# Shorter inverse roots and a new order of steps behind feed-forward layers and in two mixers

## The reference

```
h = rms_norm(x);  proj = h @ w_in
mix = (sigmoid(g_a) * (rg_lru(...) @ w_rnn_out) + sigmoid(g_b) * (sparse_attention(...) @ w_att_out)) @ w_o
x = x + rms_norm(mix)                       # post norm of the mixer: "f0"
f = (silu(h @ w_gate) * (h @ w_up)) @ w_down        # h = rms_norm(x), width 2816
x = x + rms_norm(f)                         # post norm of the feed-forward layer: "f1"
```

## Time and profile before

| | |
|---|---|
| median of 3 runs | 1452.25 us (1450.88 to 1452.64) |
| the profiled execution: its own time, its span | 1452.73 us, 1450.9 us |
| PE busy | 1406.1 us, 97% of the span |
| DVE busy | 892.9 us, 62% |
| ACT busy | 770.1 us, 53% |
| DMA | 242.57 MB, mean 167 GB/s |
| granted clock of PE, mean | 0.985 of full speed |
| chain that ended last | PE 93%, DVE 3%, ACT 3%, issue 1% |

### The profile page before, as it was taken

How to read it: one execution, slowest core, us unless ns; L and a number is a source line. 1 busy time by engine, 2 the same in 40 slices (tenths; PEclk the granted TensorE clock), 3 DMA queues, 4 the chain that set the end, 5 groups by cost and what they waited for, 6 DMA issues and landing times.

```text
span 1450.9 us, 18581 instructions
## 1 busy us (share of the span) xinstructions
PE 1406.1 (97%) x6978; PEld 1183.1 (82%) x6978; DVE 892.9 (62%) x1429; ACT 770.1 (53%) x1153; POOL 14.0 (1%) x21
## 2 busy tenths in 40 slices
PE   6999999899998999999989999999999989999999
PEld 6798888788887788888768888888888868788887
DVE  6889756755555655558876555565555684555543
ACT  5589844554544444446755444444444585554442
POOL 2000000000000000000000000000000000000000
PEclk9999999999999999999999999999999999999999
DMA  8442566476654666565445665666656422366651
GB/s 285 130 132 79 175 221 182 139 210 186 186 188 134 189 189 185 182 187 174 157 127 179 188 177 187 188 188 187 182 183 189 142 88 73 88 191 186 189 186 62
DMA packets 131767, 242.57 MB, mean 167 GB/s; under 512 B 8544, under 2 KB 21472, under 8 KB 131680
## 3 DMA queue, kind: packets, MB, share of 16 engines
q1 hardware_dynamic: 130768, 239.15, 54.1%
q0 software_dynamic: 624, 2.10, 0.5%
q10 hardware_dynamic: 288, 0.14, 0.0%
HBM read 240.31 MB, written 1.05 MB: 166 GB/s over the span
## 4 chain that ended last, share of the span: by engine, by line
PE 93%; DVE 3%; ACT 3%; issue 1%; DMA 0%; SPq 0%; ACTq 0%; DVEq 0%
PE PB L345 27%; PE PB L347 27%; PE PB L346 27%; PE PB L385 5%; PE PB L610 2%; PE PB L499 2%; PE PB L339 1%; PE PB L341 1%; PE PB L340 1%; PE PB L503 0%; ACT JK L380 0%; DMA X<-in_x_dram 0%; PE PB L791 0%; DVE XC L777 0%; PE PB L980 0%
## 5 line engine op out<-in xcount | busy, mean ns | idle before, releaser
L318 DVE TENSOR_TENSOR WL<-RAW,WH 128x1024 fp32r<-128x1024 f32 (+1 forms) x453 | 549.7, 1218 | 458.9 <-ACT WH L312 458.7
L312 ACT ACTIVATE WH<-RAW 128x1024 fp32r<-128x1024 f32 (+1 forms) x453 | 476.8, 1054 | 538.7 <-PE PB L347 530.5
L345 PE MATMUL PB<-WH,AT0h 128*128 128x512 f32 (+3 forms) x1328 | 510.8, 385 | 13.0 <-DVE AT0l L1220 6.0
L347 PE MATMUL PB<-WH,AT0l 128*128 128x512 f32 (+3 forms) x1328 | 500.5, 377 | 0.0
L346 PE MATMUL PB<-WL,AT0h 128*128 128x512 f32 (+3 forms) x1328 | 500.2, 377 | 0.0
L345 PEld LDWEIGHTS PB<-WH,AT0h 128*128 128x128 f32 x1328 | 253.5, 191 | 60.5 <-issue 16.4
L346 PEld LDWEIGHTS PB<-WL,AT0h 128*128 128x128 f32 x1328 | 253.8, 191 | 44.6 <-issue 1.9
L347 PEld LDWEIGHTS PB<-WH,AT0l 128*128 128x128 f32 x1328 | 253.0, 191 | 45.5
L345 PE MATMUL PB<-WH,FTh 128*128 128x512 f32 x440 | 172.2, 391 | 0.0
L347 PE MATMUL PB<-WH,FTl 128*128 128x512 f32 x440 | 171.3, 389 | 0.0
L346 PE MATMUL PB<-WL,FTh 128*128 128x512 f32 x440 | 171.2, 389 | 0.0
(11 more groups left out here) (301 smaller groups left out, 1059.0 us busy)
## 6 DMA issues: line engine op xcount, KB each, us to landing
RAW<-in_ffn_w_gu_dram SPq DMA_DIRECT2D x88, 512.0 KB, 3.7
RAW<-in_ffn_w_gu_2b_dram SPq DMA_DIRECT2D x88, 512.0 KB, 3.7
RAW<-in_w_in_dram SPq DMA_DIRECT2D x48, 512.0 KB, 4.3
RAW<-in_ffn_w_down_dram SPq DMA_DIRECT2D x44, 512.0 KB, 3.3
RAW<-in_ffn_w_down_2b_dram SPq DMA_DIRECT2D x44, 512.0 KB, 3.4
...
```

What stands on the lines that cost most here:

```text
L312: e.activation(WH[i % NHL][:, 0:m], RAW[i % NRAW][:, 0:m], ACT.Copy).then_inc(*up("hi", i))
L318: e.tensor_tensor(WL[i % NHL][:, 0:m], RAW[i % NRAW][:, 0:m], WH[i % NHL][:, 0:m].bitcast(F32), ALU.subtract).then_inc(*up("lo", i))
L345: e.matmul(o, p.src[0][:, kx, t], h[:, j:j + p.n], start=start, stop=False)
L347: ins = e.matmul(o, p.src[1][:, kx, t], h[:, j:j + p.n], start=False, stop=stop)
```

## The change

It rewrites the root, cuts the post norm into three pieces, and moves calls in the lists of PE, ACT and DVE. Loads, tiles and semaphores stay as they are.

The root works on the sum, not on the mean; epsilon times the width goes into the addition of the partial sums where there is one, and the scale of the query heads (64 ** -0.5) into the constants. For one value per partition the two multiplications y * y * v are one instruction.

```diff
-        def inverse_root(e, v, y, t, n, name, key):
-            e.tensor_scalar(ti, vi, 1, None, ALU.logical_shift_right)
-            e.tensor_scalar(yi, ti, -1.0, float(0x5F3759DF), ALU.mult, ALU.add)
-            for r in range(3):
-                e.tensor_tensor(t, y, y, ALU.mult)
-                e.scalar_tensor_tensor(t, t, -0.5, v, ALU.mult, ALU.mult)
-                ins = e.scalar_tensor_tensor(y, t, 1.5, y, ALU.add, ALU.mult)
-        def rstd(e, v, y, t, n, width, name, key):
-            e.tensor_scalar(v, v, 1.0 / width, EPS, ALU.mult, ALU.add)
-            inverse_root(e, v, y, t, n, name, key)
+        def root(e, v, y, t, n, factor, name, key):
+            c = (factor * 3 / 256) ** (1 / 15)
+            bits = float(0x5F3759DF - 2 ** 31 - 130000 + round(float(np.log2(c)) * 2 ** 23))
+            e.tensor_scalar(t.bitcast(I32), v.bitcast(I32), 1, None, ALU.logical_shift_right)
+            e.tensor_scalar(y.bitcast(I32), t.bitcast(I32), -1.0, bits, ALU.mult, ALU.add)
+            for r in range(2):
+                if n == 1:
+                    e.tensor_scalar(t, y, y, v, ALU.mult, ALU.mult)
+                else:
+                    e.tensor_tensor(t, y, y, ALU.mult)
+                    e.tensor_tensor(t, t, v, ALU.mult)
+                if r == 0:
+                    e.scalar_tensor_tensor(y, t, -3 * c ** 2, y, ALU.add, ALU.mult)
+                else:
+                    e.scalar_tensor_tensor(t, t, -40 / 3 * c ** 6, t, ALU.add, ALU.mult)
+                    e.scalar_tensor_tensor(y, t, 80 * c ** 12, y, ALU.add, ALU.mult)
+        def rstd(e, v, y, t, n, width, name, key, factor=1.0):
+            e.tensor_scalar(v, v, width * EPS, None, ALU.add)
+            root(e, v, y, t, n, factor * width ** 0.5, name, key)
...
         def dve_rs(e, n):
-            e.tensor_tensor(SP[n], S2[n][:, 0:2], S2[n][:, 2:4], ALU.add)
-            rstd(e, SP[n], RS[n], TM[n], 2, D, "rs", n)
+            e.scalar_tensor_tensor(SP[n], S2[n][:, 0:2], D * EPS, S2[n][:, 2:4], ALU.add, ALU.add)
+            root(e, SP[n], RS[n], TM[n], 2, D ** 0.5, "rs", n)
```

PE's list:

```diff
 # behind WO[1], f0
             pe_turn_block(e, 'f0', 0, 1)
+            dense(e, F[0][0][0], 0, 1)
             pe_turn_block(e, 'f0', 1, 0)
+            dense(e, F[0][0][0], 1, 2)
             pe_turn_block(e, 'f0', 1, 1)
-            dense(e, F[0][0][0], 0, 8)
+            dense(e, F[0][0][0], 2, 8)
```

ACT's and DVE's lists follow: `act_exp`, `act_p`, `dve_max` and `dve_diff` move to where the new order of PE needs them, with `hi` and `lo` of the chunks between them. What the text below speaks of:

```diff
 # ACT, f1
             act_squares(e, 'f1', 1, 0)
-            act_squares(e, 'f1', 1, 1)
             act_block_hi(e, 'f1', 1, 0)
+            act_squares(e, 'f1', 1, 1)
 # ACT, even mixer, end
             hi(e, 233)
-            act_p(e, AT_B, 7)
+            act_sub(e, 1)
             hi(e, 234)
-            act_sub(e, 1)
+            act_out_hi(e, 'b', 1)
             act_squares(e, 'f2', 0, 0)
-            act_out_hi(e, 'b', 1)
 # ACT, odd mixer
             act_exp(e, AT_C, 0)
-            hi(e, 381)
+            act_exp(e, AT_C, 1)
             act_p(e, AT_C, 0)
             act_ukv(e, 0, 0)
...
             act_uq(e, 1, 1)
-            act_exp(e, AT_C, 1)
+            act_p(e, AT_C, 1)
             act_exp(e, AT_C, 2)
-            act_p(e, AT_C, 1)
 # DVE, f0
             lo(e, 74)
-            dve_post(e, 'f0', 0)
+            dve_post_root(e, 'f0', 0)
             lo(e, 75)
-            dve_post(e, 'f0', 1)
+            dve_post(e, 'f0', 0, 0)
+            dve_post(e, 'f0', 0, 1)
+            lo(e, 76)
+            dve_post_root(e, 'f0', 1)
             dve_block_lo(e, 'f0', 0, 0)
+            dve_post(e, 'f0', 1, 0)
+            dve_post(e, 'f0', 1, 1)
             dve_block_lo(e, 'f0', 0, 1)
+            lo(e, 77)
 # DVE, f1
-            dve_post(e, 'f1', 0)
+            dve_post_root(e, 'f1', 0)
             lo(e, 141)
+            dve_post(e, 'f1', 0, 0)
+            dve_post(e, 'f1', 0, 1)
+            lo(e, 142)
             dve_block_lo(e, 'f1', 0, 0)
-            dve_post(e, 'f1', 1)
+            dve_post_root(e, 'f1', 1)
             dve_block_lo(e, 'f1', 0, 1)
-            dve_rs(e, 'f1')
-            lo(e, 142)
-            dve_block_lo(e, 'f1', 1, 0)
+            dve_post(e, 'f1', 1, 0)
+            dve_post(e, 'f1', 1, 1)
             lo(e, 143)
             lo(e, 144)
+            dve_block_lo(e, 'f1', 1, 0)
+            dve_rs(e, 'f1')
             lo(e, 145)
             dve_block_lo(e, 'f1', 1, 1)
 # DVE, start of each mixer (210, 211 and 370, 371)
             dve_rs(e, 'od')
+            lo(e, 371)
             dve_x_lo(e, 'od', 2)
             dve_x_lo(e, 'od', 3)
-            lo(e, 371)
```

More of the change, by code:

```diff
@@ new lines, in root @@
+                if r == 0:
+                    e.scalar_tensor_tensor(y, t, -3 * c ** 2, y, ALU.add, ALU.mult).then_inc(*up("dve"))
+                else:
+                    e.scalar_tensor_tensor(t, t, -40 / 3 * c ** 6, t, ALU.add, ALU.mult).then_inc(*up("dve"))
+                    e.wait_ge(*last("dve"))
+                    e.scalar_tensor_tensor(y, t, 80 * c ** 12, y, ALU.add, ALU.mult).then_inc(*up(name, key))
+        def rstd(e, v, y, t, n, width, name, key, factor=1.0):
+            e.tensor_scalar(v, v, width * EPS, None, ALU.add).then_inc(*up("dve"))
@@ L370, in rstd @@
             e.wait_ge(*last("dve"))
-            inverse_root(e, v, y, t, n, name, key)
-        def square(e, half, src, total, name, key):
-            e.wait_ge(*last("jk"))
-            e.activation(JK[:, half, 0:width(src)], src, ACT.Square, accum_out=total).then_inc(*up("jk", key))
+            root(e, v, y, t, n, factor * width ** 0.5, name, key)
         def cond_square(e, dst, src, total, key, scale=1.0):
@@ L3005, in dve_even_mixer @@
             dve_max(e, AT_B, 7)
+            dve_g_lo(e, 0)
+            dve_g_lo(e, 1)
+            lo(e, 228)
+            dve_diff(e, AT_B, 7)
+            dve_sub(e, 0)
+            lo(e, 229)
+            lo(e, 230)
             dve_out_lo(e, 'b', 0)
-            lo(e, 230)
-            dve_diff(e, AT_B, 7)
             lo(e, 231)
```

203 lines of the change are left out of this document (99 added, 104 removed).

## The result

The kernel after the change takes **1439.14 us** in the median of 4 runs (1437.14 to 1441.74), beside 1452.45 us before (4 runs, 1450.88 to 1453.14): a ratio of 0.9912, 95% interval 0.9899 to 0.9926. The forecast was 1438.0 in 1432.0 to 1444.5. The profiled execution took 1437.14 us with a span of 1435.3, 15.6 less than the profiled execution of before; the sum had 14.3.

What follows compares the result with a forecast made beforehand. PE, busy 97% of the span, was taken as the bound. Gains 0.6 + 0.3 + 2.8 + 5.6 + 6.0 = 15.3, less 1.0 for hand-overs, took 1452.7 to 1438.4; median 0.5 lower, 1438.0 us, range 1432 to 1444.5.

Steps and rivals of the forecast that it cites:

- A: Main case, chance 0.50: all as worked out, falls left at 29.8, f0 and 1248; 1435.5 to 1440.5 us.
- The root: Root in the norms: thirteen steps become 8 (1.54 us, 0.97 less) or 10 (0.58 less); two-pointer form taken as 0.16 us.
- Rival D: Chance 0.04: reordering only moves the waits to ACT, and only roots with PE behind them count; about 1448 us.
- The start: First norm's root, ahead of PE's first turn: three steps less, 0.6 us gained, perhaps only 0.3.
- f0: Post norm f0: pass 0 starts 2.9 us earlier, the clock's fall stays; gain 0.3 us, 3.3 without the fall.
- f1: Post norm f1: pass 2 has no wait, idle 2.0 and 1.8 us remain, pass 6 at 478.45; gain 2.8 us.
- rival B: Chance 0.25: new idle stretches in f1 and odd mixer bring one or two falls, or 1204's stays; 1441 to 1444.5 us.
- Even mixer: Even mixer's end: output's turn follows at once, pass 2.9 us earlier, no fall there (2.7 back); together 5.6 us.
- Start of the odd mixer: Odd mixer's start: lo(371), 1.0 us, goes ahead of dve_x_lo; less the root's 0.6, a loss of 0.4 us.
- Odd mixer: Odd mixer: P1 without a wait, V1 after 2.0 idle, V7 at 1205.1; 6.0 us less, 3.3 from the fall at 1204.0.
- Hand-overs: Eleven hand-overs placed at 0.05 us take up to 0.15 elsewhere in the trace: 1.0 us added.
- C: Chance 0.18: one or two falls vanish at 29.8 (3.4), f0 (3.0) or 1248 (2.8), being shifted; 1431.5 to 1435 us.

Runs made afterwards that it cites:

- e1_roots: Kernel after the change with only the shorter roots, every list in the order of the kernel before: 1446.17 us.
- e3_fill: Changed kernel plus 512-column matmuls whose results nobody reads, in PE's idle stretches at f0, f1 and the odd mixer's start and end: 1433.47 us.
- e4_lo371: Changed kernel with lo(371) moved back behind dve_x_lo at the odd mixer's start: 1435.17 us.
- e9_posts_new: Changed kernel with another order in f0 and f1: block lo ahead of root and weights' lo, f0's late turns behind more passes: 1434.06 us.
- e6_odd_old: Changed kernel with the odd mixer's lists in the order of before, lo(371) among them, short roots kept: 1439.22 us.
- e10_best: Changed kernel with the list moves of e9_posts_new and e4_lo371, plus unread matmuls at f0 and the odd mixer's start and end: 1428.39 us.
- The second profiled one: The changed kernel itself, unaltered, run and profiled once more: median 1439.38 us.
- e12_posts_only: Changed kernel with both mixers' lists as before, keeping the shorter roots and the new lists of f0 and f1: 1447.78 us.

## Why the prediction was right, point by point

The order of ends was right at every place, and the time came out 1.1 us above the forecast, inside A's own range. That it came so close is partly luck, as the points on the falls below show. One row of the kernel before, by line, bears on the first point: the same instruction with one pointer operand (`lam`).

```profile
L562 DVE TENSOR_SCALAR SM<-SM 128x1 f32<-128x1 f32 x8 | 1.7, 214 | 0.3
```

To compare instants, the lead ahead of a place is added to after's time, which gives it in before's frame.

- **The root: count right, price of one step wrong.** "I take 0.16" for the form with two pointers; it takes 0.273, beyond the other end of 0.25. The row of line 562, with one pointer, could have told that 0.16 was too little. Eight steps take 1.8 us (261.20 to 263.00) where 1.54 were said, so such a root saves 0.71 and not 0.97. That is 0.225 us a step, and one of the prediction's own signs of being wrong (over 0.2 us a step) came true. There are four such roots; it cost a few tenths of the forecast. Of the 13.6 us that go from DVE's elapsed time 10.6 are busy time, as the pages have it. Rival D had about 1448 for roots alone, e1_roots took 1446.17. Ten steps, 1129.34 to 1131.19 by the trace, take 1.85 where 1.95 were said.
- **The start: 0.6** was said; the lead at PE's first product is 0.7, and 0.4 behind it where the fall there is as long as before.
- **f0: 0.3** was said with the clock's fall kept, measured 0.5 and 0.4. Root 1 starts at 267.32 + 3.0 = 270.3 (said: 270.3), pass 0 at 270.23 + 3.0 = 273.2 (said: 273.0), behind an idle 3.24 (said: 3.1). The 6.6 passes that the prediction leaves for full rate should be 6.2 (5.9 us at half rate hold pass 0, a turn and 0.8 of pass 1), which with the turn gives its 9.1 us. e3_fill shows the other half of the sentence, 3.3 without the fall.
- **f1: 2.8** was said, 1.7 measured in both profiles. Pass 0 is at 462.01 + 3.5 = 465.5 as said, `lo` of (0,1) follows the root at once, and pass 2 has no wait. The wait ahead of pass 4 is 1.82 (said: 2.0). Pass 6 is at 479.5 and not at 478.45: the fall from 470.6 to 474.0, which is rival B's in place and in mechanism. B had 1.6 for it; it took 1.1, since the wait ahead of pass 6 shrank from 1.8 to 0.95.
- **Even mixer: 5.6** was said, 5.6 measured in both: the turn at 740.90 + 5.2 = 746.1 (said: 746.2), without a wait; the pass at 743.15 + 5.2 = 748.4 (said: 748.4), behind 1.66 of idle (said: 1.7); no fall. No new wait came of the reordering ahead of it. Of the 5.6, 2.7 are the fall at 750.0. By the table of falls this one goes with the new order (none of 10, beside 4 of 4), but what it saves isn't found again in the whole: undoing the even order cost 0.9 in the median and 1.8 in the rest, and did not raise the mean of the falls (12.9 beside 14.1).
- **Start of the odd mixer: +0.4** was said, 1.8 measured. The instant was right: 1132.75 + 10.7 = 1143.45, 0.4 behind the 1143.07 of before. The other 1.4 are the fall right behind it, at half rate until 1136.2. The step that failed is that only A's three falls were counted in the sum; B had named f1, V1 and P2 for new ones, not this place. e4_lo371 shows the cause of the wait; that the fall comes with `lo(371)` ahead is likely by the table (4 of 6, beside none of 6), and e9_posts_new shows that it needn't.
- **Odd mixer: 6.0 net** was said, with the 0.4 in it 6.4 by itself; 6.6 and 7.0 measured. P1 has no wait, V1 is at 1175.35 + 10.7 = 1186.05 and without the fall's 1.4 just where it was said (1184.65). It waits 2.37, not 2.0, and in one of the two profiles keys4 run at half rate behind it, which was B's case, though it cost 0.4 and not 2 to 3.4. V7 is, counted in the same way, at 1195.66 + 10.7 - 1.4 = 1205.0 (said: 1205.1). The fall at 1204 is gone, as said; by e1_roots and e6_odd_old it can go without the new order, and by e4_lo371 and e10_best it can come with it.
- **Hand-overs, +1.0:** can't be told. Without them the sum gives 1437.4 where the profiled execution took 1437.1, but 2.4 us of that execution's lead were luck that no step had: 0.7 because PE ran at full rate from its first product on, 1.6 from the short fall near 30 us. The second profiled one, with neither, took 1439.35, 1.0 above the sum with hand-overs; its falls in f1 and at the start of the odd mixer (1.1 and 1.4 by the first profile) are more than that.

So the number of falls in A was wrong (three left, of 6.8 us: 20.4; in the profile 27.2 in six), and the sum stood in the profiled execution because the errors were of both signs: C's gain in the first fall against B's short ones. Over all executions A's three falls would make 10.2 us in the column of falls, and the mean is 14.1. There the change brings 12.0 us of mean span where the sum had 14.3; the forecast came closer than that because it started from a profiled execution 1.2 us above the mean span of before. What the case at hand shows is a mixture of A and B: the falls are down from 19.5 us to 14.1 and not to 10.2. Of the signs named, PE waits nowhere for V's evacuation, the windows at 750.0 and 1204.0 are gone, and in place of the one at 1183.5 stands one half as long, or none.

That the falls' number would be open was argued from the rows and is now shown: of two executions of one program one fell at V1 and the other did not, and e9's idle 2.29 us ahead of line 1255 brought no fall where after's 2.28 did. The Trainium skill, TensorE: Matmul & The Clock Gate, Part 1, holds that the window of the clock's monitor runs freely and that the same kernel's slow matmuls at the start therefore vary from run to run; the runs agree as to the varying, which here goes on all through the kernel, with rests within 1428.9 to 1431.4 under spans of 1446.1 to 1453.9. That a free-running window is its cause no run here shows.

**What stays open.** Which of two equal idle stretches brings a fall can't be told from these traces. Nor is it explained why the falls of e12_posts_only come out 2.9 us above e1_roots', with less idle time; the difference is twice the error of the means (seven runs and eleven), and no run tells a cause.
